# A hybrid layer on one core: unnormalised probabilities in the first attention, with sums and weights joined at the end

## The chip, the cores and the metric

One core of one Trainium2 chip runs the whole program. The metric is the device time of one execution in microseconds (us); the time before the change is 3220.58 us, the median of three runs (3219.6 to 3220.68).

The engines named here are TensorE (PE, matrix products; PEld is its loading of weights), VectorE (DVE), ScalarE (ACT), GpSimd (POOL) and SyncE (SP). Each runs its own instructions in the order written; they meet through semaphores. Matrix products write to PSUM: here `acc`, six banks of 512 columns (`acc[:, s, p]`, two slots `s`, three banks `p`), and `aux`, two banks.

## What is computed

The program is one hybrid layer (attention, gated convolution and a recurrence side by side, then a feed-forward part) and two more layers of another kind. The change touches only the first attention: six heads of 64 columns over 1024 positions, two heads for each of three patterns (window, dilation) = (128, 1), (512, 4), (2048, 16). The reference, cut to what matters:

```python
def dilated_window_attention(q, k, v, slopes, window, dilation):
    ...   # positions regrouped by residue mod dilation, blocks of 128 queries,
    ...   # keys of the own and the previous block
    s = jnp.where(valid, s + bias, -jnp.inf)
    m = jnp.max(s, axis=-1, keepdims=True)
    p = jnp.exp(s - m)
    l = jnp.sum(p, axis=-1, keepdims=True)
    o = jnp.einsum("brhnqk,brhnkc->brhnqc", p, vb) / l
    lse = (m + jnp.log(l))[..., 0]
    ...
def attention_mixer(q, k, v):
    ...   # o and lse of the three patterns stacked
    alpha = jax.nn.softmax(lse, axis=2)
    return (o * alpha[..., None]).reshape(B, S, ATTN_WIDTH)
```

The weight of pattern g is exp(lse_g) over the sum of the three, which is exp(m_g) l_g over the same sum. So the division by l_g and the factor l_g cancel: out_g = exp(m_g) (p_g V_g) / sum_h exp(m_h) l_h.

## The kernel before, in words

Activations lie transposed in SBUF: 128 columns of the width in the partitions, positions along the free dimension, in `X` (residual, 8 chunks), `Ah`/`Al` (`act_hi`, `act_lo`, a value split in two for the products) and `R` (`work`, 19 chunks). A "unit" of the wide products takes a 128x1024 block of weights that SP loads and POOL splits (lines 418 to 422); its products are all recorded at line 472.

The first attention lies between the 19 units of the input projection and the 8 units of the output projection, and is written out by hand, with no loop on the chip and no planner. It has `PATTERN_STEPS` = 6 steps, one a head (`g, j = divmod(step, 2)`: pattern and head), each in two halves b of 4 blocks of 128 queries. Per half:

- PE `pattern_scores` (lines 738, 740; 64 partitions deep) into `acc[:, b, 0:2]`
- DVE `pattern_maxima`: scale and band (1923), a memset of blocks without predecessor (1926, 1928), the negated maxima (1929)
- ACT `pattern_exponents`: four exponentials with their sums (1334) and a logarithm (1339)
- DVE `pattern_weights`: reciprocal (1937), normalised probabilities (1939), lse (1941), lse times the identity (1942)
- PE `turn_probabilities`: transposes into `aux` (752); ACT `copy_turned` (all ACT copies have line 1166)
- PE `pattern_values` (772, 774) into 64 partitions of `acc[:, b, 2]`, and `spread_lse` (782) into the other 64
- ACT `copy_pattern_out`, and DVE `take_lse` (1954, or 1956 where the order of positions is restored)

Steps 4 and 5 have only the own block of keys, so half the columns. Values of a pattern are turned by `turn_pattern_values` (721) ahead of its two steps. The convolution's sums for its layer norm (789), its centring (1985), squares (1370), deviation (1376, 1379), norm (1965, 1966) and gates (1388, with a load of another function table on each side), and the splits of convolution and recurrence (1763, 1764) lie between the steps on the same queues. Five of the eight chunks of the output projection's input come from there.

Behind step 5 DVE and ACT join the patterns: maximum and differences (2005 to 2008), exponentials (1394), their sum (2011, 2012), its inverse (1398, 1400), and for each pattern two products and a split (2015, 2016, 1763, 1764). `wide_two` then runs the first two units chunk by chunk as `a_ready` counts them, not before five are there. Line 2021 adds a unit to the residual, which ACT has reloaded from HBM (1392) because the attention uses its place.

## Time and profile before

| | us |
|---|---|
| median of the runs | 3220.58 |
| profiled execution, time | 3221.37 |
| profiled execution, span of the core | 3219.6 |
| first transpose of values to first wide product behind the attention | 279.5 to 408.1 |
| last attention chunk ready for `wide_two` | 436.5 |

Over the span PE is busy 94%, PEld 83%, DVE 44%, ACT 23%, POOL 33%. These are averages over stages with other limits; the stage of the change is 5% of the span and shows as a dip of PE in the slices at its place. Times in the rows count from the start of the span. In a window the granted clock (PEclk) is a share of TensorE's full speed: 0.50 is 1.2 GHz, 1.00 is 2.4 GHz. The chain of waits names at each moment what the end waits for.

### The profile page before, as it was taken

What the parts mean: (1) busy time and instruction counts of PE and PEld (TensorE: products, weight loads), DVE (VectorE), ACT (ScalarE), POOL (GpSimd) and SP (SyncE); (2) the same over time, 40 slices, a digit from 0 to 9 for tenths busy, and PEclk for the clock granted to TensorE, in tenths of its full rate; (3) what the DMA queues carried; (4) which work ended last, traced back from release to release, by engine and by line L of the source; (5) the groups of instructions that cost most, each with busy time, mean ns of one, the idle gap of its engine ahead of it and who ended that gap; (6) DMA issues with size and microseconds to landing.
All of it is one profiled execution on the core that took longest, in us unless ns stands there. A gap on an engine that the chain in (4) does not pass through costs nothing.

```text
span 3219.6 us, 41152 instructions
## 1 busy us (share of the span) xinstructions
PE 3020.5 (94%) x16248; PEld 2678.1 (83%) x16248; DVE 1426.7 (44%) x1818; ACT 739.6 (23%) x1334; POOL 1070.1 (33%) x1335
## 2 busy tenths in 40 slices
PE   6988698999999998999999899999999999899999
PEld 4766576777777787999999788799999999788899
DVE  4657766222322237520022666664620022666661
ACT  2143422000000004100111555502100110555500
POOL 2523034444444443333434111134433433111132
PEclk9998799999999999999999999999999999899999
DMA  2101021111111111212112000141212212000052
GB/s 108 46 33 36 1 98 35 47 51 46 46 46 46 46 46 33 106 46 95 51 53 86 20 14 14 41 166 47 106 46 73 73 40 93 27 14 14 14 186 79
DMA packets 47445, 182.60 MB, mean 57 GB/s; under 512 B 6080, under 2 KB 6208, under 8 KB 46912
## 3 DMA queue, kind: packets, MB, share of 16 engines
q1 hardware_dynamic: 31248, 113.19, 10.6%
q10 hardware_dynamic: 16048, 67.28, 5.5%
q8 instruction: 112, 1.84, 0.2%
q14 instruction: 37, 0.30, 0.0%
HBM read 150.06 MB, written 30.39 MB: 56 GB/s over the span
## 4 chain that ended last, share of the span: by engine, by line
PE 84%; DVE 11%; ACT 3%; issue 2%; DMA 0%; POOL 0%; DVEq 0%; ACTq 0%; SPq 0%; POOLq 0%
PE acc L472 62%; PE acc L937 4%; PE aux L1053 4%; PE acc L1032 3%; PE acc L986 2%; PE acc L575 2%; PE acc L921 2%; DVE act_lo L1764 1%; DVE work L1803 1%; DVE act_lo L1796 1%; PE acc L949 1%; DVE act_hi L1763 1%; PE acc L959 1%; DVE ff_split L1764 1%; PE acc L970 0%
## 5 line engine op out<-in xcount | busy, mean ns | idle before, releaser
L400 POOL TENSOR_TENSOR w_lo<-w_raw,w_hi 128x256 fp32r<-128x256 f32 (+1 forms) x924 | 811.1, 909 | 17.2
L472 PE MATMUL acc<-act_hi,w_hi 128*128 128x348 f32 (+1 forms) x2896 | 713.3, 347 | 41.7 <-ACT residual L1260 13.2
L472 PE MATMUL acc<-act_lo,w_hi 128*128 128x348 f32 (+1 forms) x2896 | 709.6, 345 | 0.0
L472 PEld LDWEIGHTS acc<-act_hi,w_hi 128*128 128x128 f32 x2896 | 507.9, 190 | 91.5 <-issue 38.4
L472 PE MATMUL acc<-act_hi,w_lo 128*128 128x348 f32 (+1 forms) x2896 | 562.7, 344 | 0.0
L472 PEld LDWEIGHTS acc<-act_lo,w_hi 128*128 128x128 f32 x2896 | 509.1, 189 | 39.6
L420 POOL TENSOR_TENSOR small<-shape_consts 128x1 f32<-128x1 f32 x192 | 45.4, 236 | 1478.2 <-PE acc L472 1367.8
L472 PEld LDWEIGHTS acc<-act_hi,w_lo 128*128 128x128 f32 x2896 | 490.9, 188 | 39.7
L472 PE MATMUL acc<-ff_split,w_hi 128*128 128x512 f32 (+1 forms) x1376 | 309.9, 374 | 10.5 <-DVE ff_split L1764 10.5
L472 PEld LDWEIGHTS acc<-ff_split,w_hi 128*128 128x128 f32 x1376 | 246.9, 188 | 57.7 <-DVE ff_split L1764 14.7
L2021 DVE TENSOR_TENSOR residual<-acc,residual 128x1024 f32<-128x1024 f32 (+1 forms) x82 | 100.7, 1228 | 389.8 <-PE acc L472 389.8
L409 POOL CAST w_hi<-w_raw 128x1024 fp32r<-128x1024 f32 x23 | 24.8, 1079 | 630.5 <-PE acc L937 543.3
L1032 PE MATMUL acc<-ff_split 128*128 128x276 f32 (+5 forms) x864 | 208.5, 354 | 0.1
L421 POOL CAST w_hi<-w_raw 128x1024 fp32r<-128x1024 f32 x192 | 201.1, 1047 | 0.0
L1053 PE MATMUL aux<-work 128*128 128x276 f32 (+5 forms) x576 | 175.4, 400 | 0.0
L1032 PEld LDWEIGHTS acc<-ff_split 128*128 128x128 f32 x864 | 140.7, 190 | 31.7 <-issue 0.7
L1431 ACT ACTIVATE work<-acc 128x1024 f32<-128x1024 f32 x32 | 32.8, 1028 | 582.1 <-PE acc L472 574.6
L472 PE MATMUL acc<-ff_split,w_lo 128*128 128x512 f32 (+1 forms) x688 | 162.7, 373 | 0.0
L1654 ACT ACTIVATE work<-acc 128x384 f32<-128x384 f32 (+2 forms) x240 | 104.4, 436 | 223.0 <-PE acc L1032 147.3
L2070 DVE TENSOR_TENSOR work<-work 128x1024 f32<-128x1024 f32 x32 | 40.4, 1261 | 241.5 <-ACT work L1431 241.0
L2283 DVE TENSOR_REDUCE small<-acc 128x1 f32<-128x512 f32 (+4 forms) x176 | 100.7, 572 | 103.6 <-PE acc L986 59.9
L472 PEld LDWEIGHTS acc<-ff_split,w_lo 128*128 128x128 f32 x688 | 124.2, 188 | 21.9
(284 smaller groups left out, 3786.3 us busy)
## 6 DMA issues: line engine op xcount, KB each, us to landing
w_raw<-in_wstream SPq DMA_DIRECT2D x215, 512.0 KB, 3.3
spill_m<-residual ACTq DMA_DIRECT2D x2, 4176.0 KB, 13.4
spill_g<-work ACTq DMA_DIRECT2D x16, 522.0 KB, 2.7
residual<-spill_m ACTq DMA_DIRECT2D x16, 522.0 KB, 5.7
work<-spill_g ACTq DMA_DIRECT2D x16, 522.0 KB, 8.0
residual<-spill_x ACTq DMA_DIRECT2D x16, 522.0 KB, 4.2
spill_x<-residual ACTq DMA_DIRECT2D x8, 522.0 KB, 3.2
spill_x<-residual ACTq DMA_DIRECT2D x1, 4176.0 KB, 12.3
```

The lines of the kernel that those rows point to most:

```text
L400: ins = nc.gpsimd.tensor_tensor(Wl[:, s, c0:c0 + w], Wraw[:, s, c0:c0 + w], Wh[:, s, c0:c0 + w].bitcast(F32), ALU.subtract)
L421: nc.gpsimd.tensor_copy(Wh[:, s, :], Wraw[:, s, :]).then_inc(sems["w_hi_done"], 1)
L472: ins = nc.tensor.matmul(acc[0:m, s, p, 0:w], wt[:, ws, w0 + j * m:w0 + j * m + m], x[:, k, p * w:p * w + w], start=(first and t == 0), st ...
L575: ins = nc.tensor.matmul(acc[:, s, p, 0:w], wt[:, ws, k * P:k * P + P], x[:, k, p * w:p * w + w], start=(first and t == 0), stop=(end and ...
L921: ins = nc.tensor.matmul(acc_n[:, 0:w], wt[:, w_head[0], (6 + j) * P:(7 + j) * P], x[:, 6 + j, c0:c0 + w], start=(j == 0 and t == 0), stop ...
L937: ins = nc.tensor.matmul(acc_q[:, 0:w], wt[:, w_head[0], j * P:j * P + P], x[:, j, c0:c0 + w], start=(j == 0 and t == 0), stop=(j == 5 and ...
L986: ins = nc.tensor.matmul(acc_r[bank][:, 0:n], qh[:, min(P * i, LASTQ):min(P * i, LASTQ) + P], kh[:, 512 * p:512 * p + n], start=True, stop ...
L1032: ins = nc.tensor.matmul(out, k2[kt][:, c0:c0 + P], q2[qt][:, lo:lo + w], start=m == 0, stop=(m == 2 and not diag))
L1053: ins = nc.tensor.matmul(aux[:, b % 2, lo - QP * pc:lo - QP * pc + w], values(h)[:, t, :], prob(k)[:, at:at + w], start=t == 0, stop=end)
L1654: do(nc.scalar.activation(prob(k)[:, 0:w], src, ACT.Exp), "p_in")
L2021: do(vec.tensor_tensor(x, acc_view(s, pieces), x, ALU.add), f"free{s}")
L2283: do(vec.tensor_reduce(to, acc_r[rough_bank(i, p)][:, 0:n], AX, ALU.max, negate=True), "rough_max")
```

## The change

Probabilities stay unnormalised and no sum is taken by ACT. The turned values get 64 columns of ones between the two heads (`VT`, 192 columns a block, in free places of `Ah`, `Al` and `X`), so that one product of 128 output partitions gives a head's values in 64 of them and the sums of its probabilities in the other 64. The negated maxima are spread by four small products each half (`spread_maxima`, into bank `acc[0:64, b, 0]`) and taken by DVE (`take_maxima`), as are the sums (`take_sums`). The next scores wait for `max_taken` instead of `sc_free`. Values of all patterns are turned at the start. The turned probabilities have a buffer for each half. The weights of the patterns (`pattern_weights`, differences of maxima, then three exponentials) are worked out before the last step's values are there. Splits and gates of convolution and recurrence move one step on. `wide_two` waits for the last maxima, no longer for the last copies.

```diff
             def pattern_scores(step, b):
...
-                    pe.wait_ge(sems["sc_free"], 2 * (step - 1) + b + 1)
+                    pe.wait_ge(sems["max_taken"], 2 * (step - 1) + b + 1)
...
+            def spread_maxima(step, b):
+                pe.wait_ge(sems["sc_max"], 2 * step + b + 1)
+                for i in range(4):
+                    ins = nc.tensor.matmul(acc[0:64, b, 0, 128 * i:128 * i + 128],
+                                           S_[:, 16 + 4 * b + i:17 + 4 * b + i].to_broadcast([P, 64]), ident,
+                                           start=True, stop=True)
+                ins.then_inc(sems["mx_ready"], 1)
...
-                    out = acc[64 * j:64 * j + 64, b, 2, 128 * i:128 * i + 128]
+                    out = acc[:, b, 2, 128 * i:128 * i + 128]
...
-                    ins = nc.tensor.matmul(out, Vt[:, 128 * t + 64 * j:128 * t + 64 * j + 64],
-                                           PT[:, 512 + 128 * i:512 + 128 * i + 128], start=not has, stop=True)
+                    ins = nc.tensor.matmul(out, VT[g][:, t, 64 * j:64 * j + 128],
+                                           TURNED[b][:, 512 + 128 * i:512 + 128 * i + 128], start=not has, stop=True)
...
+            for g in (1, 2):
+                turn_pattern_values(g)
             pe.wait_ge(sems["conv_done"], 1)
             conv_sum((X[:, 2, :], X[:, 3, :]))
+            spread_maxima(0, 0)
             for step in range(PATTERN_STEPS):
...
+                more = step + 1 < PATTERN_STEPS
+                turn_probabilities(step, 0)
+                spread_maxima(step, 1)
+                if more:
+                    pattern_scores(step + 1, 0)
+                if step == 0:
+                    pe.wait_ge(sems["conv_squared"], 2)
+                    conv_sum((R[:, 17, :], R[:, 18, :]))
+                pattern_values(step, 0)
+                turn_probabilities(step, 1)
+                if more:
+                    pattern_scores(step + 1, 1)
+                pattern_values(step, 1)
+                if more:
+                    spread_maxima(step + 1, 0)
+            pe.wait_ge(sems["max_taken"], 2 * PATTERN_STEPS)
+            wide_two(PIECES1, (sems["a_ready"], 8), (1, 0), 5)
             pe.wait_ge(sems["av_copied"], 2 * PATTERN_STEPS)
-            wide_two(PIECES1, (sems["a_ready"], 8), (1, 0), 5)
...
             for step in range(PATTERN_STEPS):     # ACT
...
+                copy_turned(step, 0)
...
+                copy_pattern_out(step, 0)
+                copy_turned(step, 1)
+                if more:
+                    for b in range(2):
                         pattern_exponents(step + 1, b)
+                else:
+                    act.wait_ge(sems["weights_due"], 1)
+                    for g in range(3):
+                        do(nc.scalar.activation(R[:, 3 + g, 0:T1], R[:, 3 + g, 0:T1], ACT.Exp), "weights_ready")
+                copy_pattern_out(step, 1)
+                if step == 1:
                     for j in range(2):
                         act.wait_ge(sems["conv_normed"], j + 1)
                         do(nc.scalar.activation(R[:, 17 + j, 0:T1], X[:, 2 + j, 0:T1], ACT.Sigmoid), "conv_gate")
...
             for step in range(PATTERN_STEPS):     # DVE
-                for b in range(2):
-                    pattern_weights(step, b)
...
+                if more:
+                    for b in range(2):
                         pattern_maxima(step + 1, b)
-                    take_lse(step, b)
+                    take_maxima(step + 1, 0)
+                take_sums(step, 0)
+                if more:
+                    take_maxima(step + 1, 1)
+                    take_sums(step, 1)
                 if step == 0:
                     conv_norm()
                 if step == 1:
-                    conv_out()
+                    recurrent_out(0)
+                    recurrent_out(1)
                 if step == 2:
-                    recurrent_out()
+                    conv_out(0)
+                    recurrent_out(2)
+                if step == 3:
+                    conv_out(1)
+                if step == 4:
+                    pattern_weights()
+            dve.wait_ge(sems["weights_ready"], 3)
+            dve.wait_ge(sems["av_copied"], 2 * PATTERN_STEPS - 4)
+            for g in range(2):
+                weigh(10 + 3 * g, g)
+                weigh(g, g)
+            do(vec.tensor_tensor(R[:, 10, full], R[:, 10, full], R[:, 13, full], ALU.add))
+            take_sums(PATTERN_STEPS - 1, 1)
+            weigh(16, 2)
+            do(vec.tensor_tensor(R[:, 10, full], R[:, 10, full], R[:, 16, full], ALU.add), "to_act")
             dve.wait_ge(sems["av_copied"], 2 * PATTERN_STEPS)
+            weigh(2, 2)
             from_act()
             for g in range(3):
-                do(vec.tensor_tensor(R[:, 3 + g, full], R[:, 3 + g, full], top, ALU.mult))
-                do(vec.tensor_tensor(R[:, g, full], R[:, g, full], R[:, 3 + g, full], ALU.mult))
+                do(vec.tensor_tensor(R[:, g, full], R[:, g, full], top, ALU.mult))
                 split(R[:, g, full], Ah[:, 5 + g, full], Al[:, 5 + g, full], "a_ready")
```

`pattern_weights` is now five products of 128x1024 on DVE once (two minima, three differences), `take_maxima` and `take_sums` are one copy of 64x512 each, and `weigh` is one product of 128x1024. Three memsets of 128x512 write the ones. ACT's exponentials no longer have a sum, and the logarithm behind them is gone. The three exponentials, the logarithm and the inverse of the joined sum remain, once each.

## Rows read from the trace of the kernel before

**Rows 1.** The page, chain that ended last, by engine

```profile
PE 84%; DVE 11%; ACT 3%; issue 2%; DMA 0%; POOL 0%; DVEq 0%; ACTq 0%; SPq 0%; POOLq 0%
```

**Rows 2.** Windows: start:end, length, busy PE, PEld, DVE, ACT, POOL, then PEclk

```profile
322.30:346.60 24.30, 16.06 (x92) 13.62 (x92) 17.61 (x22) 11.62 (x29) 0.00 (x0) 0.71 0.00 1
346.60:370.60 24.00, 14.82 (x84) 12.57 (x84) 17.92 (x22) 8.61 (x24) 0.00 (x0) 0.71 0.00 1
```

**Rows 3.** Waits, 279.5 to 440: total us, times, longest

```profile
PE aux L752 <- DVE residual L1939: 30.0, 5, 8.7
```

**Rows 4.** Timeline of PE: start, us, line, operation; 1.2 and 2.4 GHz

```profile
286.90 6.06 PE L789 MATMUL acc<-residual,shape_consts 128*128 128x512 f32 x8
...
308.99 0.40 PE L772 MATMUL acc<-work,residual 128*64 128x128 f32 x2 [1.30 <-ACT work L1376]
...
323.80 1.97 PE L752 MATMUL aux<-shape_consts,residual 128*128 128x128 f32 x8 [7.04 <-DVE residual L1939]
333.32 1.09 PE L752 MATMUL aux<-shape_consts,residual 128*128 128x128 f32 x8
374.01 2.07 PE L740 MATMUL acc<-work 64*128 64x128 f32 x8
389.01 1.16 PE L740 MATMUL acc<-work 64*128 64x128 f32 x8
395.00 0.76 PE L774 MATMUL acc<-residual 128*64 128x128 f32 x5 [1.68 <-ACT residual L1166]
```

**Rows 5.** Groups of DVE, shapes apart, 279.5 to 440: busy us, mean ns

```profile
L1939 DVE TENSOR_TENSOR residual<-residual,small 128x1024 f32<-128x1024 f32 x8 | 9.8, 1225 | 0.3
L1929 DVE TENSOR_REDUCE small<-residual 128x4 f32<-128x1024 f32 x8 | 9.8, 1220 | 0.3
L1956 DVE COPY work<-acc 64x512 f32<-64x512 f32 x8 | 8.4, 1055 | 11.6 <-PE acc L782 11.4
L1763 DVE CAST act_hi<-work 128x1024 fp32r<-128x1024 f32 x6 | 4.2, 694 | 0.2
L1965 DVE SCALAR_TENSOR_TENSOR residual<-residual,params,work 128x1024 f32<-128x1024 f32 x2 | 2.6, 1284 | 0.1
L1928 DVE MEMSET residual<- 128x256 f32 x4 | 1.1, 272 | 0.5
```

**Rows 6.** Timeline of ACT: exponential, its sum, the table, the gates

```profile
333.00 0.50 ACT L1334 ACTIVATE residual<-residual,small 128x256 f32<-128x256 f32 x1
333.40 0.19 ACT L1334 ACTIVATION_READ_ACCUMULATOR residual<-residual,small 128x1 f32 x1
...
320.19 1.28 ACT L1388 ACT_TABLE_LOAD   x1
321.48 2.01 ACT L1388 ACTIVATE work<-residual 128x1024 f32<-128x1024 f32 x2
342.37 1.09 ACT L1166 ACTIVATE residual<-aux 128x512 f32<-128x512 f32 x2
```

**Rows 7.** Windows at either clock, columns as in rows 2

```profile
279.50:291.50 12.00, 11.96 (x46) 8.99 (x47) 11.59 (x11) 4.23 (x10) 6.07 (x4) 0.58 0.14 44
310.00:316.00 6.00, 6.00 (x51) 5.06 (x51) 1.84 (x2) 3.56 (x12) 0.00 (x0) 1.00 0.00 1
386.00:398.00 12.00, 6.53 (x45) 4.46 (x44) 8.74 (x17) 8.81 (x26) 0.00 (x0) 1.00 0.00 0
```

**Rows 8.** Timeline behind step 5, DVE, ACT and PE

```profile
410.59 3.74 DVE L2008 TENSOR_TENSOR work<-work 128x1024 f32<-128x1024 f32 x3
...
414.80 2.96 ACT L1394 ACTIVATE work<-work 128x1024 f32<-128x1024 f32 x3 [7.73 <-DVE work L2008]
...
427.52 0.73 PE L472 MATMUL acc<-act_hi,w_hi 128*128 128x512 f32 x2 [3.88 <-DVE act_lo L1764]
...
436.54 0.73 PE L472 MATMUL acc<-act_hi,w_hi 128*128 128x512 f32 x2 [1.43 <-DVE act_lo L1764]
```

**Rows 9.** DMA issues, 240 to 480: count, KB, us to landing

```profile
residual<-in_xT ACTq DMA_DIRECT2D x1, 4096.0 KB, 13.5
```

More of the change, by code:

```diff
@@ L179, in build @@
         G_, _ = place("pool_split", 8 * RW, F32R, offset=r_at + 4 * 8 * RW)
+        Y_ = tuple(place(f"spare{i}", 2 * TP + 1024, offset=-(-(o + 4 * 5 * TP) // 32) * 32)[0] for i, o in enumerate((ah_at, al_at)))
         assert at[0] <= nc.sbuf_usable_end, (at[0], nc.sbuf_usable_end)
@@ L327, in build @@
         PATTERN_STEPS = 2 * len(PATTERNS)
-        PROBS = (X[:, 1, 0:1024], X[:, 4, 0:1024])
-        def turned(step):
-            return (R[:, 1, :] if step < 2 else X[:, 3, :])[:, 0:1024]
+        PROBS = (X[:, 4, 0:1024], X[:, 5, 0:1024])
+        TURNED = tuple(t[:, 1536:2560] for t in Y_)
+        VT = tuple(t[:, 0:1536].rearrange("p (t c) -> p t c", c=192) for t in Y_ + (X_,))
+        assert 1536 <= 2 * TP
         def parts_of(g):
@@ L758, in pattern_values @@
                 g, j = divmod(step, 2)
-                PT = turned(step)
                 pe.wait_ge(sems["pt_copied"], turns(step, b))
@@ L1347, in copy_turned @@
                     act.wait_ge(sems["pt_ready"], c["pt_ready"].value())
-                    do(copy(turned(step)[:, 512 * part:512 * part + 512], aux[:, part, :]), "pt_copied")
+                    do(copy(TURNED[b][:, 512 * part:512 * part + 512], aux[:, part, :]), "pt_copied")
             def copy_pattern_out(step, b):
@@ L1392, in _ @@
             act.dma_start(X[:, :, META:T2], xT.rearrange("(c p) t -> p c t", p=P)).then_inc(sems["xre_in"], 16)
-            for g in range(3):
-                ins = nc.scalar.activation(R[:, 3 + g, 0:T1], R[:, 3 + g, 0:T1], ACT.Exp)
-                do(ins, "to_dve" if g == 2 else "act_step")
-            c["to_act"].step()
-            act.wait_ge(sems["to_act"], c["to_act"].value())
-            do(nc.scalar.activation(R[:, 6, 0:T1], R[:, 6, 0:T1], ACT.Ln))
+            do(nc.scalar.activation(R[:, 6, 0:T1], R[:, 10, 0:T1], ACT.Ln))
             after()
@@ L1909, in _ @@
                 free[n % 2].step()
+            dve.wait_ge(unit.sem, unit.value())
             dve.wait_ge(sems["bands_in"], 16)
@@ new lines, in take_maxima, with take_sums @@
+            def take_maxima(step, b):
+                g, j = divmod(step, 2)
+                dve.wait_ge(sems["mx_ready"], 2 * step + b + 1)
+                to = R[64 * j:64 * j + 64, 3 + g, full]
+                do(in_order(step, (to[:, 512 * b:512 * b + 512], to, b), acc[0:64, b, 0, :]), "max_taken")
+            def take_sums(step, b):
+                g, j = divmod(step, 2)
+                dve.wait_ge(sems["av_ready"], 2 * step + b + 1)
+                to = R[64 * j:64 * j + 64, 10 + 3 * g, full]
+                do(in_order(step, (to[:, 512 * b:512 * b + 512], to, b),
+                            acc[64 * (1 - j):64 * (1 - j) + 64, b, 2, :]), "sum_taken")
@@ L1989, in _ @@
             for step in range(PATTERN_STEPS):
[L1990 to L1993 removed]
+                more = step + 1 < PATTERN_STEPS
+                if more:
+                    for b in range(2):
                         pattern_maxima(step + 1, b)
[L1995 removed]
+                    take_maxima(step + 1, 0)
[3 more added lines that the diff above has]
+                    take_sums(step, 1)
                 if step == 0:
```

160 lines of the change are left out of this document (60 added, 100 removed).

## The prediction

> **What bounds the kernel now.** I read the page first: the chain that ended last runs 84% through TensorE and 11% through DVE [rows 1], so a change on other engines counts only where TensorE waits for them. Then the windows of the two middle steps of the attention: in 24.3 and 24.0 us TensorE is busy 16.1 and 14.8, DVE 17.6 and 17.9, ACT 11.6 and 8.6, at a mean granted clock of 0.71 [rows 2]. No engine is full. The stage is a round of handovers, scores, maxima, exponentials, normalisation, transposes, with both halves of a step treated one after the other by each engine, and by that clock more than half of the time is at 1.2 GHz. The waits name the place: the transposes wait 30.0 us in total for the normalised probabilities of line 1939, up to 8.7 at a time [rows 3]. DVE reaches line 1939 only after the copies of lse and the splits of convolution and recurrence. Behind the last step comes a serial piece, 28.4 us from DVE's end of the lse copies to the last chunk (408.1 to 436.5 [rows 8]), and the end of the stage is the last chunk's products, from 436.54 on.
>
> All of this is TensorE idle or slow in front of work that it must do in any case, so what the stage gets shorter, the kernel gets shorter. Nothing behind it is known to absorb it, except the reload below.
>
> **What the change does to each part.** Removed from DVE, each half: line 1939's product of 1.23 us on the path [rows 5], two tiny operations and a reciprocal, and the product with the identity, half as wide. The lse copy is replaced by that of the sums, of equal shape. Removed from ACT: the sum that follows each exponential and the logarithm. Added to DVE: one more copy each half, 1.06 in patterns 2 and 3 (line 1956), 0.7 in the first; three memsets of 512 columns once, by 0.27 for 256 in line 1928 [rows 5] about 0.5 each, 1.5 in all. They lie under the first convolution sums, which keep DVE waiting for more than that; without that cover they would cost 1.5. Added to TensorE: four spreading products each half instead of one of equal columns, so nothing but loads. The value products load 128 columns instead of 64; the scores' loads are 128 wide already and eight passes take 1.16, against 0.76 for five value passes [rows 4], so I take 0.12 a pass where the trace has 0.11 (bounds 0.11 and 0.14: 0 to 1 us a step). The scores' new wait for the copied maxima puts behind it, on TensorE, the values of the same half and the next transposes.
>
> I now lay the new order out engine by engine from these durations and follow what comes last. Steps on DVE are 0.035 apart, so 1.26 for 1.225 and 0.73 for 0.69.
>
> (a) *Start to the first values.* Sixteen transposes move ahead of the convolution sums, at 1.2 GHz 1.97 for eight [rows 4], and the second group waits 0.8 for ACT's copies. So the first sums, which began at 286.9, begin at 291.6 and take 6.06 [rows 4]: 297.7. Centring in four pieces and the first maxima copy take 5 x 0.73 on DVE: 301.3; scores 1.8, second sums 3.4 at 2.4 GHz (6.06 at 1.2), the logarithm of the first half 0.6: **307.2**, against 308.99 now [rows 4]. At the low clock it is 310.
>
> (b) *First values of step 0 to those of step 1.* Here TensorE itself is full. One half at 2.4 GHz: transposes 1.0, scores 16 passes 1.8, values 16 passes 1.95, spreading 8 passes 0.9, together 5.65 and **11.3** for a step (at 1.2 GHz about 22, by 1.97 and 2.07 for eight [rows 4]).
>
> (c) *Step 1 to 2.* Longest is DVE, then ACT: the norm of the convolution 4.2 (2 x 1.31 for line 1965, and 2 x 0.79 for the operation with one tensor behind it, near the 0.73 of the cast in line 1763 [rows 5]), both maxima with a memset 2 x 2.9 [rows 5], the last four exponentials 1.7 (0.40 from start to start [rows 6], with no sum between), the copy of values 0.5, table, gates, table 1.28 + 2.01 + 1.28 [rows 6], two copies of turned probabilities 1.1 [rows 6]. The gates stand on ACT ahead of the copies that the values wait for. With hops of 0.3 and what DVE lags: **17.6**.
>
> The trace has the first gate starting 1.29 after its table load began, so no more than the load itself [rows 6]. The Trainium skill, ScalarE: Activation LUTs, section "What ACT_TABLE_LOAD costs", puts a drain of about 1.38 behind each load, 2.66 together. By that rule (c) would be 2.8 longer; the row decides, and I add nothing.
>
> (d) *Step 2 to 3.* TensorE is the longest again, and behind the wait of (c), about 5 us, it has dropped to 1.2 GHz for one stretch as it does now after idling. Values 3.9, transposes 1.1, scores 1.8, values 1.95, spreading 0.9, transposes 1.0, spreading 0.9, scores 0.9 (half as many now), a wait of 1.1 for exponentials and copies: **13.6**.
>
> (e) *Step 3 to the weights of patterns.* DVE is busy without a gap: gate product and two splits 1.26 + 2 x 2.0 = 5.3, two half-wide maxima 2.9, four copies 4.35, gate product and split 3.25, maxima 2.9, copies 4.35, hops and waits 1.1 [rows 5]: **24.1**.
>
> (f) *Weights to the last chunk.* Five products 6.3 (three now take 3.74), three exponentials 2.96 + 0.1 [rows 8], four weightings, a sum, the last sums' copy, a weighting, a sum: 7 x 1.26 + 1.09 = 9.9, logarithm and exponential 2.2, then for each pattern a product and a split, 3 x 3.25 = 9.8: **31.3**. It is longer than the 28.4 of now, but begins in step 5 and not behind it. A pattern costs 3.25 where it cost 4.5.
>
> (g) *Last chunks on TensorE.* Chunks 6, 7 and 8 come at 398.7, 402.0 and 405.2. TensorE has idled 9 us before chunk 6, which then runs at 1.2 GHz, as at 427.52 now: 4.3, then 2 x 2.8 for the others. End 3.3 behind the last chunk. That the first five chunks start before the last copies is worth nothing by itself: they need 14 us and there are 23 before the sixth chunk is there (now also they ended 3.9 before it [rows 8]).
>
> Sum: 307.2 + 11.3 + 17.6 + 13.6 + 24.1 + 31.3 + 3.3 = 408.4. Now that point is 436.54 + 3.1 = 439.7. The gain is **31 us**. The profiled execution took 3221.37, 0.8 above the median 3220.58; 3221.4 - 31.3 = 3190, and against the median **3189**.
>
> One cover gets thin. The reload of the residual takes 13.5 us [rows 9]; it is issued when DVE has the joined sum, then at 393, lands at 406.6, and line 2021 wants it when the first unit is done, at about 407. Now it has 10 us to spare. If it lands later the price is 0 to 2 us.
>
> **The rivals.**
>
> *Clock at 2.4 GHz throughout.* Then (a) ends at 304, (d) is 11.6, and (g) 3.0; in all 5 to 7 less: 3182. For it: 310 to 316 is full at 1.00, and 386 to 398 stays at 1.00 with TensorE busy only 6.5 of 12 us [rows 7]. Against it: the 5 us wait in (c).
>
> *Handovers don't interleave.* In (b) and (d) TensorE's 11.3 equals the chain of one half: values 1.95, transposes 1.0, scores 1.8, maxima 2.9, exponentials 1.7, copies 1.6, hops 0.3, makes 11.3. The scores also wait for the copied maxima, which DVE takes only behind the maxima of the other half. If both add by some 3 us a step over five steps, the gain halves: 3204. For it: in the kernel now no engine is more than 75% busy in a step [rows 2]. Against it: the most serial link, normalisation behind the splits, is gone.
>
> *Clock at 1.2 GHz throughout (slower than before).* Mechanism: half of TensorE's time is transposes and score products, and these don't bring the clock up. For it: from 279.5 to 291.5 it is busy 11.96 of 12 us, mostly such work, at a mean of 0.58 [rows 7]. Price: (a) 316 because the spreading and all handovers there stretch too, then three steps of 22, one of 17 and one of 11 to the last step's values, 2 to the weights, 31.3 and 3.3, makes 316 + 66 + 17 + 11 + 2 + 34.6 = 447, 7 to 8 later than now: 3228. It decides only if the low clock holds in nearly all of (a) to (e); if it holds in half, 3207. Against it: 310 to 316, the same mixture at 1.00 [rows 7].
>
> Transposes at 2.4 GHz are in the trace, eight in 1.09 [rows 4]. The Trainium skill, TensorE: Matmul & The Clock Gate, "Part 4: PE-mode transpose", says that transposes don't count as busy for the clock. By that rule this rival is the case to fear, since a quarter of a step is transposes; the rows at 1.00 speak for a clock that, once up, stays up through them.
>
> *The change doesn't do what it says:* the weights could still end last because the last sums' copy waits for the last values. They come at 374 to 376 and the copy is wanted at 389, so this has 13 us of cover. I give it nothing of its own.
>
> **How the numbers follow.** Forecast as laid out, 3183 to 3197: 0.62. High clock: 0.12. No interleaving, 3197 to 3210: 0.18. Half-low clock or an unnamed stall, 3207 to 3226: 0.04. Low clock, slower: 0.04. Range 3180 to 3205, which leaves out under 2 in 10. Measurement tells 0.2%, 6.4 us: faster means under 3214.1. Faster 0.93, same 0.03, slower 0.04.
>
> **What would show it.** After: wide products behind the attention begin near 375 instead of 408, in two bursts with some 9 us between chunk 5 and chunk 6; last chunk at 405; PEclk of 310 to 372 mostly 1.00; values of successive steps start 11, 18, 14, 12, 10 us apart; ACT's copy behind the gates ends the longest wait of TensorE inside the steps; the idle before line 1939 is gone. The forecast is wrong if steps of the first pattern take over 14 us with TensorE idle, if a copy of maxima or sums is what scores or values wait for, or if line 2021 waits for the DMA.

## The result: 25 us faster, and the profile after

| | before, us | after, us |
|---|---|---|
| median of the runs, four each on one chip | 3220.63 (3219.6 to 3221.51) | 3195.54 (3194.88 to 3196.22) |
| ratio, 95% interval | 1 | 0.9922 [0.9905, 0.9939] |
| profiled execution, time | 3221.37 | 3196.22 |
| its span, mean granted clock | 3219.6, 0.977 | 3194.4, 0.985 |
| first transpose of values to end of the first two units | 279.54 to 439.60: 160.1 | 281.12 to 413.25: 132.1 |

The kernel is faster, by 25.1 us; 31 was forecast, and 3195.5 lies in the forecast's own 3183 to 3197. "End of the first two units" is the end of their last product, where the sum of the prediction ended; the next unit begins 0.1 to 0.2 us later.

The page of the changed kernel, the chain that ended last by engine. Against [rows 1] TensorE's share is 3 points less and DVE's 3 more: where the end waits in the stage, it now waits for DVE more than before.

```profile
PE 81%; DVE 14%; ACT 3%; issue 2%; DMA 1%; DVEq 0%; POOL 0%; ACTq 0%; SPq 0%; POOLq 0%
```

Windows of the changed kernel, cut at the starts of the terms (b) to (g); columns as in [rows 2]:

```profile
309.00:321.00 12.00, 11.74 (x96) 10.81 (x96) 5.47 (x7) 8.05 (x17) 0.00 (x0) 1.00 0.01 2
321.00:339.00 18.00, 12.37 (x99) 10.97 (x97) 17.21 (x19) 11.34 (x18) 0.00 (x0) 0.88 0.00 0
339.00:353.00 14.00, 13.79 (x88) 12.52 (x88) 8.00 (x9) 7.03 (x14) 0.00 (x0) 0.78 0.01 1
353.00:378.00 25.00, 19.42 (x136) 16.41 (x136) 23.22 (x27) 13.18 (x28) 0.00 (x0) 0.93 0.00 1
378.00:413.00 35.00, 24.97 (x104) 19.96 (x104) 28.37 (x25) 6.67 (x7) 1.00 (x2) 0.85 0.35 135
```

The bound alternates as the prediction laid it out: TensorE is full in the first (11.74 of 12) and third (13.79 of 14), DVE in the second (17.21 of 18), the fourth (23.22 of 25) and, with waits for ACT, the last. In [rows 2] no engine was above three quarters.

Waits of TensorE from 281 to 413: us in total, times, longest. Nothing is left of the 30.0 us of [rows 3]; the transposes wait for exponentials, 1.7 in all.

```profile
PE acc L472 <- DVE act_lo L1770: 9.5, 1, 9.5
PE acc L779 <- ACT spare L1173: 5.7, 3, 4.9
PE acc L746 <- DVE small L1936: 4.2, 3, 2.1
PE acc L736 <- DVE work L1943: 2.3, 1, 2.3
...
PE aux L760 <- ACT residual L1340: 1.7, 4, 0.7
```

The line of 2.3 us is a wait of the scores for a copy of maxima (line 1943), which the prediction named as a sign of being wrong. It comes once, at 299.38, in front of step 1's first scores, where the sum of (a) had counted that copy; no scores wait for one in the steps behind it.

### The profile page after: what moved, and what is told of

Same layout as the page of the kernel before. It is cut to its first block, busy times and chain, and to the rows that moved or that the text cites. A ratio compares the mean times of both kernels' runs of the same rounds, so it can differ in the third digit from the quotient of the medians.

```text
span 3194.4 us, 41207 instructions
## 1 busy us (share of the span) xinstructions
PE 3008.1 (94%) x16320; PEld 2675.1 (84%) x16320; DVE 1419.0 (44%) x1790; ACT 731.1 (23%) x1275; POOL 1072.8 (34%) x1335
## 4 chain that ended last, share of the span: by engine, by line
PE 81%; DVE 14%; ACT 3%; issue 2%; DMA 1%; DVEq 0%; POOL 0%; ACTq 0%; SPq 0%; POOLq 0%
PE acc L472 60%; PE acc L944 4%; PE aux L1060 4%; PE acc L1039 3%; PE acc L993 2%; PE acc L928 2%; PE acc L575 1%; DVE work L1809 1%; DVE act_lo L1802 1%; DVE residual L2176 1%; DVE residual L1879 1%; PE acc L956 1%; DVE act_lo L1770 1%; DMA spill_x<-residual 1%; PE acc L966 1%
## 5 line engine op out<-in xcount | busy, mean ns | idle before, releaser
L472 PEld LDWEIGHTS acc<-ff_split,w_hi 128*128 128x128 f32 x1376 | 246.9, 188 | 57.7 <-DVE ff_split L1770 14.7
```

Source lines behind the costliest of these rows:

```text
L472: ins = nc.tensor.matmul(acc[0:m, s, p, 0:w], wt[:, ws, w0 + j * m:w0 + j * m + m], x[:, k, p * w:p * w + w], start=(first and t == 0), st ...
```

## The experiments

Each kernel ran beside the kernel before on its chip, in three sets; medians of before were 3219.19, 3218.68 and 3220.48. "Stage" is always the length from the first transpose of values to the end of the first two units, read from the trace; it is 160.1 before and 132.1 after. "Values" are the starts of the first values of a step behind the first transpose: before 29.4, 49.9, 74.2, 96.5, after 28.1, 40.0, 57.7, 72.2, 84.3, 94.5.

Three theories of the gain stood against each other. *Place (Q):* what cost was where the normalisation stood in DVE's queue, between the exponentials and the transposes, behind copies and splits. *Operation (O):* the removed operations cost their own length and no more. *Clock (C):* the handovers cost because TensorE idles and then runs at 1.2 GHz.

### One part alone: normalisation out, nothing else moved

```diff
-                pe.wait_ge(sems["pr_ready"], 2 * step + b + 1)
+                pe.wait_ge(sems["sc_exp"], 2 * step + b + 1)
...
-                do(vec.reciprocal(S_[:, 44 + 4 * b:48 + 4 * b], S_[:, 24 + 4 * b:28 + 4 * b]))
-                rl = S_[:, 44 + 4 * b:48 + 4 * b].unsqueeze(2).to_broadcast([P, 4, 256 - lo])
-                do(vec.tensor_tensor(pb, pb, rl, ALU.mult), "pr_ready")
```

The turned probabilities of steps 2 to 5 also get a place of their own, so that nothing else has to wait.

> The kernel before, in which DVE no longer multiplies the probabilities by the inverse of their sum (lines 1937 and 1939 left out; the attention's output is then not divided by the sums, so it is another value) and the transposes wait for the exponentials alone; the turned probabilities of steps 2 to 5 get a place of their own. Everything else keeps its order. Theory Q (the queue): what cost the time was that the transposes waited behind everything in DVE's queue, copies, norm and splits; laid out by the durations of before, the last lse copy ends near 385 instead of 408, so 3197 to 3200. Rival O (the operation): only its own 1.26 + 0.2 us counts, once or twice a step, 6 to 9 us in all, so 3212 to 3215. Rival C (the clock): TensorE stays at 1.2 GHz for as long as now, and the gain is under 12: above 3208.

Measured: 3199.19 us (3196.19 to 3199.7), ratio 0.9942 [0.9925, 0.9958], 20 us under before. The wide products begin 107.6 us after the first transpose instead of 128.6, and the stage is 138.7. Three quarters of the change's gain in the stage, 21 of 28 us, come with this one edit. Timeline of TensorE in this kernel (start, us, line, operation): at 322.51 the transposes follow the last product in front of them with no idle time noted, where [rows 4] has 7.04 us in front of the same transposes.

```profile
321.68 0.90 PE L783 MATMUL acc<-residual,shape_consts 128*64 128x512 f32 x1
322.51 1.09 PE L753 MATMUL aux<-shape_consts,residual 128*128 128x128 f32 x8
```

Eight products of 1.23 us [rows 5] and four of half the width, 0.69 each, are 12.6 us of DVE, and the twelve reciprocals that go with them, 0.18 each, 2.2 more. Of these 14.8 us at most the ones in front of which TensorE waits can count. The gain is larger than all of them together: O falls. What goes is the time that the product stood behind other work. The time at 1.2 GHz falls too, from 75 us of the stage to 48 (added up from the granted clock of windows of 2 us), so this run alone doesn't tell Q from C.

### The clock held up in the kernel before

```diff
+                if step < 3:
+                    pe.wait_ge(sems["av_copied"], 2 * step + 1)
+                    pe.wait_ge(sems["lse_taken"], 2 * step + 1)
+                    for _ in range(6 if step == 0 else 7):
+                        nc.tensor.matmul(acc[:, 0, 2, :], ident, C_[:, 0:512], start=True, stop=True)
```

> The kernel before, with six or seven idle products of 512 columns on TensorE (into a bank that is free then) behind steps 0, 1 and 2, where it now waits 7 to 9 us and falls to 1.2 GHz; nothing else changes. They last 5 to 6 us at 2.4 GHz, less than the gap. Rival C: the clock is what the change brought back; three stretches of 8.5 us at 1.2 GHz become 4.3, about 12 us less: 3208. Theory Q: TensorE's low clock lies partly beside DVE's copies and maxima; the schedule laid out with the clock high in steps 1 and 2 ends 3 us earlier: 3217 to 3218, within 2 us of that. PEclk of the windows from 319 to 357 must be 1.00 for the test to hold.

Measured: 3220.18 us (3216.42 to 3225.89, ten runs), ratio 1.0008 [0.9999, 1.0018]: no difference. Windows, first two rows before, then with the idle products:

```profile
343.00:357.00 14.00, 8.89 (x42) 8.13 (x42) 10.71 (x15) 1.88 (x4) 0.00 (x0) 0.52 0.00 0
357.00:367.00 10.00, 5.93 (x45) 4.43 (x42) 7.20 (x8) 7.19 (x22) 0.00 (x0) 0.99 0.01 2
```

```profile
343.00:357.00 14.00, 10.42 (x71) 7.72 (x69) 12.17 (x16) 4.57 (x13) 0.00 (x0) 0.99 0.01 2
357.00:367.00 10.00, 9.29 (x28) 5.62 (x29) 6.00 (x8) 4.01 (x12) 0.00 (x0) 0.67 0.00 0
```

The idle products raise the clock from 0.52 to 0.99 in one stretch, and it falls to 0.67 in the next, where it had been 0.99. So the condition was met in part only: values of steps 1 to 3 come 1.8, 3.5 and 3.1 us earlier (48.1, 70.7, 93.4), and the first wide product at 128.8, not earlier at all. What the clock gives in this round of handovers, some 3 us, is lost again at the end of it. Over the whole stage the time at 1.2 GHz is 58 us instead of 75, and the stage is 160.2 us against 160.1: 17 us less at the low clock brought nothing. C as the main cause falls; a kernel with the clock at 1.00 throughout was not reached.

### The product put back into the changed kernel

A product by ones on DVE, `product(step, b)`, stands again between exponentials and transposes; it changes no value.

```diff
-                pe.wait_ge(sems["sc_exp"], 2 * step + b + 1)
+                pe.wait_ge(sems["pr_ready"], 2 * step + b + 1)
...
+            def product(step, b):
+                dve.wait_ge(sems["sc_exp"], 2 * step + b + 1)
...
+                do(vec.tensor_tensor(pb, pb, one, ALU.mult), "pr_ready")
...
             for step in range(PATTERN_STEPS):     # DVE
...
+                product(step, 1)
                 if more:
                     for b in range(2):
                         pattern_maxima(step + 1, b)
...
                 take_sums(step, 0)
                 if more:
+                    product(step + 1, 0)
                     take_maxima(step + 1, 1)
```

So the second half's product stands at the start of a step, behind all the work of the step before, and the first half's behind the next maxima, a copy of maxima and `take_sums(step, 0)`.

> The changed kernel with one DVE product of each half's probabilities (by ones, so the result is the same) put between the exponentials and the transposes again, as early in DVE's queue as the order allows. Theory Q: the transposes are behind DVE's queue again, each step gets the wait for splits, norm and copies back, and TensorE's low clock with it; laid out by the durations, the stage ends 38 to 42 us later than in the changed kernel: 3233 to 3237, slower than the kernel before. Rival O: 12 products of 1.26 or 0.7, of which what is on the path adds 6 to 13 us: 3202 to 3209.

Measured: 3231.63 us (3226.94 to 3237.38), ratio 1.0041 [1.0025, 1.0057]: slower than before the change, and 36 us above the changed kernel for 12.6 us of DVE. The stage is 169.7, 37.6 longer than in the changed kernel. The wait of TensorE, 279 to 440, then DVE's timeline around one product:

```profile
PE aux L760 <- DVE residual L2001: 40.3, 10, 7.4
```

```profile
327.79 1.28 DVE L1967 SCALAR_TENSOR_TENSOR residual<-residual,params,work 128x1024 f32<-128x1024 f32 x1
329.11 0.75 DVE L1968 TENSOR_SCALAR residual<-residual,params 128x1024 f32<-128x1024 f32 x1
329.89 1.23 DVE L2001 TENSOR_TENSOR residual<-residual,shape_consts 128x1024 f32<-128x1024 f32 x1
```

The 40.3 us answer to the 30.0 of [rows 3]: the same product, again behind the convolution's work in the queue. Together with the first experiment this shows it from both sides: taking it out of the old order gives 21 us of the stage, putting it into the new one costs 37.6. Why it costs more there was not tested; the new order has more in the queue that waits for it and that it waits for (the copies of maxima and sums, and with them the next scores).

### The gates ahead of the exponentials, and without gates

In the changed kernel the one long wait inside the steps is 4.86 us in front of the values at 338.84. Timeline of TensorE, then of ACT:

```profile
338.84 0.80 PE L779 MATMUL acc<-spare,spare 128*128 128x128 f32 x2 [4.86 <-ACT spare L1173]
```

```profile
333.09 1.28 ACT L1399 ACT_TABLE_LOAD   x1
334.39 2.00 ACT L1399 ACTIVATE work<-residual 128x1024 f32<-128x1024 f32 x2
336.41 1.28 ACT L1177 ACT_TABLE_LOAD   x1
337.71 1.08 ACT L1173 ACTIVATE spare<-aux 128x512 f32<-128x512 f32 x2
```

Two table loads and two gates, 4.6 us together, stand ahead of the copies that the values need. But ACT had idled before the exponentials in front of them, waiting for maxima:

```profile
327.85 1.71 ACT L1340 ACTIVATE residual<-residual,small 128x256 f32<-128x256 f32 x4 [2.97 <-DVE small L1936]
330.75 1.71 ACT L1340 ACTIVATE residual<-residual,small 128x256 f32<-128x256 f32 x4 [1.20 <-DVE small L1936]
```

The edit puts the block there:

```diff
                 copy_turned(step, 1)
+                if step == 1:
+                    for j in range(2):
+                        act.wait_ge(sems["conv_normed"], j + 1)
+                        do(nc.scalar.activation(R[:, 17 + j, 0:T1], X[:, 2 + j, 0:T1], ACT.Sigmoid), "conv_gate")
+                    log_and_exp()
                 if more:
                     for b in range(2):
                         pattern_exponents(step + 1, b)
...
-                if step == 1:
...
-                    log_and_exp()
```

> The changed kernel with the two gates and their two table loads moved ahead of the exponentials of step 2 on ACT, where ACT waits 3 us for the maxima, from behind them. Term (c) said that the 4.6 us of table, gates, table stand in front of the copies that TensorE waits 4.9 us for. Theory: the exponentials start 1.6 later, the copies 3 earlier, and the idle before the values of step 2 goes from 4.9 to 2 or less; TensorE may then stay at 2.4 GHz, worth 1 to 2 more; DVE's gap-free piece behind it takes part of this back. 3191 to 3194, middle 3192.5. Rival: DVE's queue alone sets the pace from step 2 on, and the gates had cover: 3195 to 3196.

Measured: 3189.99 us (3189.35 to 3193.27), ratio 0.9918 [0.9902, 0.9935]; stage 128.2, 3.9 shorter. Timeline of ACT there, then one line of TensorE: the block lies where ACT idled, and the exponentials behind it make the transposes wait 2.27 us; the wait of 4.86 is gone.

```profile
322.19 1.28 ACT L1391 ACT_TABLE_LOAD   x1
323.48 2.00 ACT L1391 ACTIVATE work<-residual 128x1024 f32<-128x1024 f32 x2
325.50 1.28 ACT L1177 ACT_TABLE_LOAD   x1
326.80 3.30 ACT L1340 ACTIVATE residual<-residual,small 128x256 f32<-128x256 f32 x8
```

```profile
328.56 1.97 PE L760 MATMUL aux<-shape_consts,residual 128*128 128x128 f32 x8 [2.27 <-ACT residual L1340]
```

The floor for this is a kernel without the gates.

> The changed kernel with the gates of the convolution and their two table loads left out (the convolution's result is multiplied by another tensor, so it is another value). It gives the floor for moving them. Theory: the 4.6 us stood on the path once, the exponentials of step 2 then wait for DVE's maxima alone, and the stage is 4 to 6 us shorter than in the changed kernel: 3189.5 to 3191.5, at most 2 below gates_early (3190). If moving them had left much on the path, it would be 3187 or less. Rival: a part of what gates_early gained lies outside the stage (its stage began 2 us earlier), and then this run shows 3192 to 3193.

Measured: 3190.36 us (3189.43 to 3190.61), ratio 0.992 [0.9904, 0.9937], stage 127.8. So the same 4.6 us, put early, cost 0.4 in the stage, which is less than two traces of one kernel differ by (1 us, below): early, they cost nothing that shows.

### The first two units late

```diff
             pe.wait_ge(sems["max_taken"], 2 * PATTERN_STEPS)
-            wide_two(PIECES1, (sems["a_ready"], 8), (1, 0), 5)
             pe.wait_ge(sems["av_copied"], 2 * PATTERN_STEPS)
             pe.wait_ge(sems["sum_taken"], 2 * PATTERN_STEPS)
+            wide_two(PIECES1, (sems["a_ready"], 8), (1, 0), 5)
```

> The changed kernel with the waits for the last copies (av_copied, sum_taken) put back ahead of the first two output units. The prediction said that the early start is worth nothing by itself. In the changed kernel's trace the last copy of sums ends at 394.6 because DVE puts it behind the weightings, and the products of five chunks take 14.1 us from 379.5. Theory: they now run from 394.6 to 408.7, past chunk 6 at 403.0, and the pair of units ends at 417 instead of 413.2, 4 us later: 3199.5 (3198.5 to 3200.5). Rival (the prediction's sentence): no difference, 3195 to 3196.

Measured: 3199.84 us (3198.53 to 3200.89), ratio 0.9951 [0.9934, 0.9967]. Timelines of DVE and TensorE in this kernel:

```profile
390.01 1.23 DVE L2035 TENSOR_TENSOR work<-work 128x1024 f32<-128x1024 f32 x1
391.26 1.00 DVE L1944 COPY work<-acc 64x512 f32<-64x512 f32 x1
```

```profile
392.48 1.19 PE L472 MATMUL acc<-act_hi,w_hi 128*128 128x512 f32 x2 [15.07 <-issue]
```

TensorE waits 15.07 us. The trace names no releaser ("issue"), but the product starts 0.22 us behind the end of DVE's copy of the last sums, for which the edit makes it wait, and that copy stands behind the weighting of two patterns. The five chunks, begun at the low clock, then end 16 us later, at 408.6, where the sixth is split at 400.7; there is no wait in front of it any more, and the stage is 137.7, 5.6 longer.

### The weights one place later

```diff
-                if step == 4:
-                    pattern_weights()
+            pattern_weights()
```

> The changed kernel with pattern_weights (five products on DVE) called behind the last step instead of in step 4's place. In the trace they start at 377.9 and the copy of the last step's first sums follows at 384.2. Theory: only that copy of 1.07 moves ahead of them, so the stage is about 1 us longer: 3196 to 3197. Rival: the early weights are what hides 6.3 of DVE and 3.0 of ACT behind the last step, and their loss costs 4 to 9: 3199 to 3204.

Measured: 3197.69 us (3196.57 to 3199.35), ratio 0.9945 [0.9928, 0.9961]; the interval overlaps that of the changed kernel. In its trace the stage is 133.5: chunk 6 starts 122.3 us after the first transpose instead of 121.9, and the low clock lasts three groups of products longer behind it. Putting one copy of sums ahead of the weights costs about 1.4 us in the stage, near the scatter of single traces. The rival (the loss of the early weights costs 4 to 9 us) did not come, but it was hardly put to the test: the edit moves the weights by that one copy, and they begin 97.2 us after the first transpose instead of 96.8, still ahead of the copy of the last sums. What it is worth to have them early at all stays open.

### The clock held up in the last gap

Ten idle products (twenty passes) stand in front of chunk 6, on top of early gates.

```diff
+                    if fill and k == 5:
+                        pe.wait_ge(sems["av_copied"], 11)
+                        pe.wait_ge(sems["sum_taken"], 11)
+                        for _ in range(fill):
+                            nc.tensor.matmul(acc[:, 0, 2, :], ident, C_[:, 0:512], start=True, stop=True)
```

> gates_early with ten idle products of 512 columns on TensorE between the fifth and the sixth chunk of the first two output units, where it waits 9.5 us and falls to 1.2 GHz. Theory: they last 8.5 us at 2.4 GHz, the sixth chunk's products take 2.8 instead of 4.4, and the end comes 1.3 to 1.6 earlier: 3188.5 (3187.8 to 3189.3). Rival: the copies that gate them, or a clock that has already dropped, make the filling run past the sixth chunk: 3190 to 3193.

Measured: 3190.24 us (3186.83 to 3190.92), ratio 0.9921 [0.9904, 0.9937], beside 3189.99 for early gates alone in another set. That left it open, and so did every other comparison across sets. The third set took four kernels to one chip.

### Four kernels on one chip

> The changed kernel as it is, beside the three variants of this set on one chip, because the earlier comparisons lie in different sets. Theory (the stage lengths in the traces carry over to the time): the same stage as seen, 132.1 us from the first transpose of values to the end of the first unit, give or take 0.5, and a time that is the zero point of this set, 3195 to 3197 if the kernel before reads 3219 to 3221. Rival (kernels of different sets can't be compared to better than 4 us, and the 5.5 us between this kernel and the one with early gates is of that kind): it reads 3189 to 3192, level with it.

> Gates ahead of the exponentials of step 2, once more, on one chip with the changed kernel. Theory: the wait of 4.86 us of the values behind the gates is what goes, the stage is 3.9 us shorter in the trace (128.2 against 132.1), so the time is 3.5 to 5.5 us under that of the changed kernel in this set. Rival (the gain in the stage is given back behind it, or was the set's): within 1.5 us of it.

> The waits for the last copies ahead of the first two units, once more, on one chip with the changed kernel. Theory: the wide products start when DVE has copied the last sums, at 113 us after the first transpose instead of 98.4, and their first five chunks, 15 us, then end behind the sixth chunk's split (120.7): the end of the first unit is 5.5 us later in the trace and the time is 4 to 5.5 us above that of the changed kernel in this set. Rival, my prediction's sentence (an early start is worth nothing by itself): within 1 us.

> Early gates and, in the wait before the sixth chunk, ten groups of idle products that keep the clock up; once more, against early gates alone in the same set. In the first traces the clock behind the gap was 1.00 up to 478 us with the idle products and 0.94 in the first 20 us without them. Theory (the clock in the gap costs): chunk 6 runs 2.8 us instead of 4.3, so the time is 1 to 2 us under that of early gates alone. Rival (what is saved at the gap comes back as a stretch of low clock elsewhere in the run): within 0.7 us of it.

| beside before at 3220.48 | median, us | ratio, interval | stage in the trace |
|---|---|---|---|
| changed | 3193.81 (3191.71 to 3194.3) | 0.9916 [0.9902, 0.9929] | 133.1 |
| early gates | 3187.92 (3187.48 to 3192.7) | 0.9899 [0.9883, 0.9914] | 128.8 |
| units late | 3200.12 (3198.53 to 3202.61) | 0.9936 [0.9922, 0.9949] | 138.3 |
| early gates and idle products | 3188.46 (3186.38 to 3190.97) | 0.9898 [0.9883, 0.9914] | 129.4 |

Early gates are 5.9 us under the changed kernel and late units 6.3 above it, by the medians of one set; the traces put 4.3 and 5.2 in the stage. One of the four runs with early gates reads 3192.7, above the lowest of the changed kernel, so its gain rests on the other three, on the first set and on the two traces together. The changed kernel read 1.2 below what its expectation allowed and its stage was 1.0 longer than in the first trace, so a single trace is good to about 1 us here. The kernel with early gates is faster than both.

The idle products gain nothing, though they did what they were put there for. TensorE's timeline with early gates alone, and then, from their first run, with the idle products:

```profile
397.24 1.22 PE L472 MATMUL acc<-act_hi,w_hi 128*128 128x512 f32 x2 [9.52 <-DVE act_lo L1770]
398.26 1.05 PE L472 MATMUL acc<-act_lo,w_hi 128*128 128x512 f32 x2
```

```profile
387.95 8.74 PE L508 MATMUL acc<-shape_consts 128*128 128x512 f32 x20
397.63 0.73 PE L472 MATMUL acc<-act_hi,w_hi 128*128 128x512 f32 x2 [0.93 <-DVE act_lo L1775]
...
400.88 0.74 PE L472 MATMUL acc<-act_hi,w_hi 128*128 128x512 f32 x2 [0.21 <-DVE act_lo L1775]
```

Chunk 6 starts 118.2 us after the first transpose in both, since DVE's split sets it, and runs at 2.4 GHz instead of 1.2 with the idle products. But DVE hands on a chunk every 3.25 us, and one takes 2.8 at the high clock: TensorE then waits for chunks 7 and 8 too, as at 400.88, and the end moves from 128.2 to 127.8 only; in the second pair of traces it is 128.8 and 129.4, so even this 0.4 is within the scatter. Neither theory had it right: the gain didn't come back as low clock elsewhere, all but 0.4 of it was never on the path. A first execution at 3186.83 had looked like a gain of 3 us.

## Why the prediction was right, and by how much its steps were off

| step | forecast, us | measured, us |
|---|---|---|
| (a) first transpose to first values | 27.7 | 28.1 |
| (b) step 0 to 1 | 11.3 | 11.8 |
| (c) step 1 to 2 | 17.6 | 17.8 |
| (d) step 2 to 3 | 13.6 | 14.5 |
| (e) step 3 to the weights | 24.1 | 24.6 |
| (f) weights to the last split | 31.3 | 31.6 |
| (g) last chunks | 3.3 | 3.7 |
| sum | 128.9 | 132.1 |

The measured ends are 309.26, 321.08, 338.84, 353.30, 377.92, 409.51 and 413.25.

**The sum.** Every step is within 1 us and every one is too short; together they lack 3.2. The stage gained 28.0, not 31.3. The rest of the gap to 25 lies in code that the change doesn't touch: the stage began 1.6 us later than before (281.12 against 279.54), and what lies behind it took 2781.2 us against 2780.0. Both are scatter of single executions: in the second trace of the changed kernel the stage begins at 279.97 and the rest takes 2779.0, and over the kernels that share the front part the start varies from 278.9 to 281.1. The gain in the third set, 26.7 by the medians, fits.

**(a)** The total was right and its parts were not: the first sums ran at 2.4 GHz in 3.60 and the second ones mostly at 1.2 GHz in 6.43, the forecast having it the other way round. In the second trace the first ones took 5.44 and the step 29.1. Where the low stretch falls in this step differs between executions of one kernel; neither trace reached the 30.5 us that the prediction gave for the low clock (310). The memsets took 0.48 each, forecast 0.5, under those sums.

**(b)** TensorE was full as said. The term that was mis-sized is that of scores and spreading: 16 score passes took 1.97 from start to start, where 1.8 was put, and eight spreading passes 1.01, where 0.9 was. Timeline of TensorE, one half:

```profile
316.05 1.09 PE L746 MATMUL acc<-shape_consts,small 128*64 128x128 f32 x8
317.06 1.09 PE L760 MATMUL aux<-shape_consts,residual 128*128 128x128 f32 x8
318.09 1.09 PE L746 MATMUL acc<-shape_consts,small 128*64 128x128 f32 x8
319.10 0.48 PE L736 MATMUL acc<-work 64*128 64x128 f32 x2
...
321.08 0.49 PE L779 MATMUL acc<-spare 128*128 128x128 f32 x2
```

Within a group the passes are 0.11 apart, as I had it, but each change to another kind of product adds about 0.1 (the first pair of scores takes 0.33, the others 0.22), and a step has eight such changes, half of which my figures left out. [rows 4] could have shown it: the eight passes in 1.16 at 389.01 are followed by the next product 1.08 behind their start and not 0.9, and I took the 0.11 alone. The value passes with loads of 128 columns took 1.86 to 1.99 for 16, forecast 1.95, so the load's width costs nothing, the lower bound of what was allowed.

**(c)** DVE, then ACT, ended it, and the copy behind the gates ended TensorE's longest wait, both as written. But the 17.6 is luck in part: the terms listed for it add up to 17.9, and to 18.2 with the hops. In the trace they are 18.1 from the start of DVE's norm, which began 0.35 before the first values, and that makes the 17.8. The second table load ended at 337.69 and the copy behind it began at 337.71. So no drain follows a load in this kernel; the 2.8 us that the Trainium skill's rule (ScalarE: Activation LUTs, "What ACT_TABLE_LOAD costs"; an estimate, two drains of about 1.38 us) would have added are not in the trace, nor in the kernels with early gates, whose load of 322.19 and gate of 323.48 are 1.29 apart. What the prediction did not ask is whether the block had to stand there. That was worth 4 to 6 us.

**(d)** Off by 0.9. TensorE is busy 13.79 of 14 at a mean clock of 0.78: of the 1.1 of waiting that was counted 0.5 came, and the passes took more, since the low stretch (334.8 to 345) covers the first 6 us of the step.

**(e) and (f)** DVE went from start to end as laid out, 0.5 and 0.3 slow. Timeline of DVE, the weights, what ACT's exponentials hold up, the last sums and the first split:

```profile
377.92 1.23 DVE L1985 TENSOR_TENSOR work<-work 128x1024 f32<-128x1024 f32 x1
...
387.26 5.01 DVE L1993 TENSOR_TENSOR work<-work 128x1024 f32<-128x1024 f32 x4 [1.98 <-ACT work L1394]
...
393.56 1.00 DVE L1944 COPY work<-acc 64x512 f32<-64x512 f32 x1
...
401.06 0.69 DVE L1769 CAST act_hi<-work 128x1024 fp32r<-128x1024 f32 x1
```

The piece starts 96.8 us behind the first transpose; before, it began two operations ahead of the 410.59 of [rows 8], at 408.1, 128.5 behind it. So the gain in (f) is its place, not its length, as said.

**(g)** 3.7 for 3.3: chunk 6, after 9.47 us idle, ran its first three of six pairs at 1.2 GHz and part of the fourth. The prediction gave the chunk 4.3 us "as at 427.52 now", and it took 4.4; but the line of [rows 8] doesn't show a low clock, since its pair takes 0.73, as the one at 436.54 does at 2.4 GHz. The low clock comes behind it, 1.05 a pair, and that chunk took 4.5. Timeline of TensorE, changed kernel, then before:

```profile
403.06 1.22 PE L472 MATMUL acc<-act_hi,w_hi 128*128 128x512 f32 x2 [9.47 <-DVE act_lo L1770]
```

```profile
428.82 1.05 PE L472 MATMUL acc<-act_hi,w_lo 128*128 128x512 f32 x2
```

The fill experiment adds that DVE's 3.25 a chunk is the bound behind it, so that this low stretch costs about 0.4 and not 1.5. The wide products began at 379.5, 98.4 us behind the first transpose, where the prediction's sign was "near 375", 95.5; chunk 6 was not held up by that.

**What failed: "worth nothing by itself".** The prediction's step was that the early start of the units brings nothing because five chunks need 14 us and 23 are there before the sixth. That counted from the last values, at 376. Without the early start TensorE would wait for the last copies, and DVE's copy of the sums was put at 389 by the prediction's own rival on the last sums. 389 + 1 + 14 is 404, 5 behind the 398.7 given for chunk 6, and three chunks of 2.8 on top end at 412.4 against 408.4: its own numbers held a price of 4 us. Measured: 5.6 and 5.2 in the stage, 6.3 in the time. The forecast did not suffer, since the changed kernel has the early start.

**The reload** had thin cover, as said: issued at 397.12, 13.0 to landing by the row below (at about 410.1 us), first used at 411.99. So 1.9 us were left, and the 0 to 2 us of price were not called on.

```profile
residual<-in_xT ACTq DMA_DIRECT2D x1, 4096.0 KB, 13.0
```

**The rivals.** *High clock throughout* fell: 31 us of the stage still ran at 1.2 GHz (300.6 to 307.4, 334.8 to 345, 372.3 to 375.7, 396.2 to 406.4), against some 75 before. In the second trace of the same kernel it is 41, with a stage 1.0 longer. *Handovers don't interleave* fell: window 309 to 321 has TensorE busy 11.74 of 12. *Low clock throughout* fell too. From 309 to 334 the clock stayed at 1.00 through a mixture of which transposes are a sixth (16 passes of the 96 of a step; the prediction had put a quarter), eight of them in 1.04 to 1.09. By the Trainium skill's rule (TensorE: Matmul & The Clock Gate, "Part 4: PE-mode transpose") transposes don't count as busy; in this trace that did not bring the clock down, and no run here shows a stretch of transposes alone. *The last sums' copy* was no stall: it stands at 393.56 in DVE's queue, with no wait in front.

**The mechanism.** "The most serial link, normalisation behind the splits, is gone" is shown by two experiments, one from each side. That it is most of the gain, 21 of 28 us, was not in the prediction as a number. The other 7 are what the order of the new kernel adds. Without the early units it loses 5 of its own stage; how the 7 split is not shown, since each part was taken away alone and from another order.

## What to carry to other kernels

An operation on the path between two engines costs its place in the queue first and its length second: here 12.6 us of DVE products (14.8 with their reciprocals) were worth 21 us in one order and 37.6 in another, and a block of 4.6 us on ACT cost 4 to 6 us in one place and nothing that shows in the gap ahead of it. When a bound is removed by algebra, list what else stands in front of each handover and move that too. Before an idle engine is kept warm, ask what hands it the next piece: if that is slower than the engine at its high clock, as here with 3.25 us a chunk against 2.8, the clock is worth next to nothing.

## What the runs showed of the hardware that I had not expected

- Idle products hold the granted clock at 1.00 through a 9.5 us gap, so that the pair of products behind it takes 0.73 instead of 1.22. In the round of handovers before the change they moved the low stretch to the next window (0.52 and 0.99 became 0.99 and 0.67), took 17 us of low clock out of the stage, and the time stayed.
- A product that loads 128 columns and one that loads 64 are the same 0.11 us a pass at 2.4 GHz in pairs (two start 0.22 apart from the next two: line 781 of the changed kernel with 128 columns, 0.39 long, and line 774 of the kernel before with 64, 0.38 long).
- Four exponentials of 128x256 take 1.71 us without their sums, where each sum had a record of 0.19 of its own [rows 6].
- The kernel before had single runs from 3211.66 to 3221.76 in two of the sets, with medians within 2 us of each other. A difference below about 4 us needed kernels on one chip with several runs each; one execution 3 us shorter told nothing.
